# Second-kind layers: where the halves of the modulation shift are made, and how far the sums of squares follow the rest tiles

## The chip, the cores and the metric

One core of a Trainium2 chip runs the kernel. Its engines work in parallel, each through an instruction queue of its own, strictly in order: TensorE (PE) for matmuls, VectorE (DVE), ScalarE (ACT), GpSimd (POOL), and SyncE (SP), which issues the weight loads. They wait for each other through semaphores only. The metric is the time of one execution in microseconds (us) on the device.

## The reference

512 tokens of width 1024 pass through two layers of a first kind (differential and dilated attention, SwiGLU) and then two of a second kind, which are the ones concerned here:

```python
for l in range(DEPTH):                       # second_block
    mod = c_act @ w_mod[l] + b_mod[l]
    sh1, sc1, gt1, sh2, sc2, gt2 = jnp.split(mod[:, None, :], 6, axis=-1)
    h = rmsnorm(x, g_mix[l]) * (1.0 + sc1) + sh1
    z = h @ w_in[l]
    ...   # y_a pooling, y_b banded attention, y_c sparse attention (top 128 keys), y_d latent attention
    mix = group_rmsnorm(jnp.concatenate([y_a, y_b, y_c, y_d], axis=-1), g_group[l])
    x = x + gt1 * (mix @ w_out[l])
    h = rmsnorm(x, g_ffn[l]) * (1.0 + sc2) + sh2
    f = (jax.nn.silu(h @ ffn_w1[l]) * (h @ ffn_w3[l])) @ ffn_w2[l]
    x = x + gt2 * f
```

`sh2` is the modulation shift that the change is about. The sparse attention selects, for each query, the 128 keys with the highest index scores.

## The kernel before

Activations lie transposed, 128 features by 512 tokens a tile, eight tiles (`KT`) for the width of 1024. Each fp32 weight chunk of 128x1024 is loaded to a ring (`wring`), and split into a high part, copied by ACT (`cut_high`, L422), and a rest, made by POOL (`cut_rest`, L445: wring - wHi). Each product of `gemm` is then three matmuls, hHi x wHi, hHi x wLo and hLo x wHi (L470). ACT makes a high part as soon as the tile that used the buffer two chunks before is done (`follow`). PSUM results go in rings of two slots: `psG` (ring G), `psT` (T), and the two score slots of `psS` (ring S). A matmul into a slot first waits until the former content has been read (`is_free`).

A second-kind layer does the following, in this order, on every engine:

1. **Front.** Twelve tiles of z (`Z_FRONT`), among which the index scores are computed on PE, rectified on ACT (`index_relu`) and summed into `score` on DVE (`index_sum`, L2405). The last two front tiles hold values, which ACT copies to `vT` (L2094). Behind the front tiles ACT loads the table of the exponential (L2140).
2. **Mixing stage.** A loop over 29 steps, written out on each engine. In step s PE computes the scores of pair s (`scores`, L1854, two slots), transposes the probabilities of pair s-2 (L1869) and multiplies those of pair s-3 by the values (L1889); steps 0 to 4, 7 and 9 hold one more z tile each (`TILE_AT`). DVE adds the bias to the scores of pair s, with the row's minimum (`lowest`, L2466), which empties the slots; ACT takes the exponential (`expo`, L2152). Between these DVE does the selection: 48 rounds (`take`), each a top-8 search (L2412) and a replacement (L2413), nine of them ahead of step 0 (`TAKEN_FIRST`), the others spread over steps by a table (`TAKE_AT`). In step 7 DVE makes two reciprocals (`c_inv`, L2525), which PE spreads (L1949).
3. **Out tiles and rest tiles.** The product with `w_out` is split over k: "out" tiles over six of the eight k tiles, within the last steps, and eight "rest" tiles over the last two (six matmuls each), when the last attention output is there. DVE adds each result to `xT` (`add_out`, L2450). ACT squares each finished tile (`norm_act_squares`, L549, two buffers `sq`), and PE adds the squares of tile j up (`squares_of(j)`, L558) behind rest tile j+1.
4. **Shift row.** PE multiplies the shift with the first two weight chunks of the FFN (L1995, L1996), for which the shift stands in `shift` as two columns for each k: its high half, copied by ACT (L2219), and the remainder, subtracted by DVE (L2531).
5. **FFN.** Gate, up and down products, PE almost without a pause.

The copy and the subtraction stand, before the change, behind the mixing loop: on ACT behind the load of the square root's table (L2213), on DVE ahead of the first rest tile's add. `modc`, from which they are made, is ready at the layer's start.

Of the kernel before, what the change touches and what calls it, by code (L numbers as in the profile page):

```python
# [25 lines left out]
ACT = mybir.ActivationFunctionType  # L26
ALU = mybir.AluOpType
# [7 lines left out]
KT = DM // P  # L35
# [96 lines left out]
def head_pair(n):  # L132

    return n // (TT - 1), 1 + n % (TT - 1)
# [108 lines left out]
def program(nc, t, out):  # L243
    ctx = ExitStack()
    with ctx:
        def sb(name, shape, where=ctx, dtype=F32):
            return where.enter_context(nc.sbuf_tensor(name, shape, dtype))
# [8 lines left out]
        def sem(name):  # L256
            return ctx.enter_context(nc.semaphore(name))
# [26 lines left out]
        shift_full, shift_row, shift_col = sem("shift_full"), sem("shift_row"), sem("shift_col")  # L284
# [171 lines left out]
        def gemm(pe, u, c, rhs, kts, i=None, Ku=0, Kc=0, start=True, stop=True, ready=None, used=True, cut=None):  # L456

            pe.wait_ge(w_cut[c % CUTS], c // CUTS + 1 if i is None else i * (Kc // CUTS) + (c // CUTS + 1))
            if start:
                pe.wait_ge(*G.is_free(u, i, Ku))
            hi, lo = rhs
            wh, wl = (wHi[:, c % CUTS, :, :], wLo[:, c % CUTS, :, :]) if cut is None else cut
            for j, k in enumerate(kts):
                for n, (w, r) in enumerate(((wh, hi), (wl, hi), (wh, lo))):
                    if ready is not None and n != 1:
                        pe.wait_ge(*ready(j)[n // 2])
                    mm = pe.matmul(psG[:, G.slot(u), :], w[:, k, :], r(j),  # L470
                                   start=start and j == 0 and n == 0, stop=stop and j == len(kts) - 1 and n == 2)
            if used:
                mm.then_inc(G.filled(u) if stop else w_used, 1)
# [23 lines left out]
        def tiles(a, first=0):  # L497
            return lambda j: a[:, first + j, :]
# [56 lines left out]
        def quarter_sums(pe, tt, parts, start=True, stop=True):  # L555
            for a in range(TT):
                for j, s in enumerate(parts):
                    mm = pe.matmul(psT[32 * a:32 * a + 32, T.slot(tt), 0:P], ones[:, 0:32], s[:, a * P:(a + 1) * P],  # L558
                                   start=start and j == 0, stop=stop and j == len(parts) - 1)
            return mm  # L560
# [1132 lines left out]
        shift = sb("shift", [P, KT, 2], blk, F32R)  # L1693
# [3 lines left out]
        modc, gains = sb("modc", [P, MODS], blk), sb("gains", [P, 2, KT], blk)  # L1697
# [35 lines left out]
        for l in range(DEPTH):  # L1733
            with nc.Block() as block:
# [42 lines left out]
                def _(pe):  # L1777
# [196 lines left out]
                    def squares_of(j):  # L1974
                        if j == 0:
                            pe.wait_ge(*T.is_free(t_N2))
                        pe.wait_ge(sq_full, q_N2 + j + 1)
                        quarter_sums(pe, t_N2, (sq[:, (q_N2 + j) % 2, :],), j == 0, j == KT - 1)\
                            .then_inc(sq_used if j < KT - 1 else T.filled(t_N2), 1)
# [3 lines left out]
                    for j in range(KT):  # L1983
                        at = 2 * (j % 4)
                        gemm(pe, g[f"rest{j}"], CH2_WR + j // 4, (tiles(hHi, REST_K[0]), tiles(hLo, REST_K[0])), (at, at + 1))
                        if j >= 1:
                            squares_of(j - 1)

                    first = (wHi[:, CH2_GU % CUTS, :, :], wLo[:, CH2_GU % CUTS, :, :]), first_cuts[0]
                    pe.wait_ge(shift_full, 2)  # L1990
# [69 lines left out]
                def _(act):  # L2060
# [28 lines left out]
                    def tile(name):  # L2089
                        u = g[name]  # L2090
                        if name in (6, 15, 16):
                            n = (6, 15, 16).index(name)
                            act.wait_ge(*G.is_full(u))
                            act.activation(vT[:, n % 2, :], psG[:, G.slot(u), :], ACT.Copy).then_inc(vT_full, 1)  # L2094
                            act.wait_ge(vT_full, n + 1)
                            act.sem_inc(G.emptied(u), 1)
                        elif name == 7:
                            act.wait_ge(*G.is_full(u))
                            for b, out in ((0, ik), (64, sak)):
                                for at in (0, 64):  # L2100
                                    ins = act.activation(out[at:at + 64, :], psG[b:b + 64, G.slot(u), :], ACT.Copy)
                            ins.then_inc(G.emptied(u), 1)
                        else:
                            if name == 17:
                                act.wait_ge(scale_full, 1)
                            copy(name, place[name], scale=-0.125 if name in (11, 12, 17, 18) else 1.0)
                        follow(act, CH2_Z + z_pos[name], u)

                    def value_rows(name):
                        u = tr[name]  # L2110
                        act.wait_ge(*T.is_full(u))
                        if name == "v6":
                            s = psT[:, T.slot(u), :].rearrange("p (c d) -> p c d", c=TT)
                            act.activation(Vsa[:, :, 0:64], s[:, :, 0:64], ACT.Copy)
                            act.activation(iws[:, :, :], s[:, :, 64:64 + IDX_HEADS], ACT.Copy,
                                           scale=(IDX_HEADS ** -0.5) * (IDX_DIM ** -0.5)).then_inc(T.emptied(u), 1)
                        else:
                            hd = 0 if name == "v15" else 2
                            act.activation(Vca[:, :, hd:hd + 2, 0:64], psT[:, T.slot(u), :].rearrange("p (c h d) -> p c h d", c=TT, h=2),
                                           ACT.Copy).then_inc(T.emptied(u), 1)  # L2120

                    def index_relu(n):
                        nk = P * (head_pair(n // 2)[1] + 1)
                        act.wait_ge(*S.is_full(s_IDX + n))
                        if n >= 4:
                            act.wait_ge(relu_used, n - 3)
                        act.activation(relu[:, n % 4, 0:nk], psS[:, S.slot(s_IDX + n), 0:nk], ACT.Relu).then_inc(S.emptied(s_IDX + n), 1)

                    for at, name in enumerate(Z_ORDER[:Z_FRONT]):
                        first, second = INDEX_AT.get(at, (None, None))  # L2130
                        if first is not None:
                            index_relu(2 * first)
                            index_relu(2 * first + 1)
                        tile(name)
                        if at == 3:
                            value_rows("v6")
                        if second is not None:
                            index_relu(2 * second)
                            index_relu(2 * second + 1)
                    act.preload_act_table(ACT.Exp)  # L2140

                    def out_T(p):
# [30 lines left out]
                    for s in range(STEPS + 1):  # L2173
# [29 lines left out]
                        if s in (5, 6):  # L2203
                            j, name = s - 5, ("CQ", "CK")[s - 5]
# [10 lines left out]
                    def rough(j):  # L2215

                        act.activation(hHi[:, j, :], xT[:, j, :], ACT.Copy, scale=gains[:, 1, j:j + 1]).then_inc(rough_high, 1)

                    act.activation(shift[:, :, 0], modc[:, 3 * KT:4 * KT], ACT.Copy).then_inc(shift_full, 1)  # L2219

                    def added(j):
                        if j in (1, 2):
# [140 lines left out]
                def _(dve):  # L2363
# [66 lines left out]
                        did(dve.memset(score[0:CHUNK, qt - 1, P * (qt + 1) - CHUNK:P * (qt + 1)], NEG))  # L2430
                    dve.wait_ge(ca_in, 16)
                    did(dve.memset(T_tab[0:CHUNK, :, SEQ - CHUNK:SEQ], FAR))
                    taken = 0
                    for _ in range(TAKEN_FIRST):
                        take(taken)
# [91 lines left out]
                        if s in DONE_AT:  # L2527
                            mix(DONE_AT[s])
                    assert taken == ROUNDS * (TT - 1)
                    dve.wait_ge(shift_full, 1)  # L2530
                    dve.tensor_tensor(shift[:, :, 1], modc[:, 3 * KT:4 * KT], shift[:, :, 0], ALU.subtract).then_inc(shift_full, 1)  # L2531

                    def rough(j):

                        dve.wait_ge(rough_high, j + 1)
                        dve.scalar_tensor_tensor(hLo[:, j, :], xT[:, j, :], gains[:, 1, j:j + 1], hHi[:, j, :], ALU.mult, ALU.subtract)\
                           .then_inc(rough_rest, 1)
# [259 lines left out]
```

## Time and profile before

| | |
|---|---|
| median of the runs before | 3213.44 us (3209.69, 3213.44 and 3215.41) |
| the profiled execution | 3212.82 us, span of the trace 3211.0 us |
| busy share of the span | PE 98%, DVE 45%, ACT 42%, POOL 43% |
| mean granted TensorE clock | 0.996 of full speed |
| second-kind layers in the trace | about 1924 to 2564 us and 2564 to 3211 us |
| mixing stage, first of them | about 2013 to 2176 us; rest tiles from there to about 2195 us |

A row of a timeline has the start and the duration in us, the engine, the source line, the operation, the tile written and those read, the shape and a count; square brackets give the engine's idle time before it and what ended it. Starts and durations are those of one profiled execution.

### The profile page before, as it was taken

To read this page: it belongs to the slowest core of one execution; us is meant where nothing else is said; L and a number is where in the kernel's file an instruction comes from. 1 tells how busy PE (TensorE), PEld (TensorE's weight loads), DVE (VectorE), ACT (ScalarE), POOL (GpSimd) and SP (SyncE) were. 2 spreads that over 40 slices of the span, in tenths; PEclk is the share of its full clock that TensorE was granted. 3 is DMA by queue.
4 is the path that set the end of the run, shared out by engine and by line. 5 is a ranking of instruction groups with operands and counts; after the bars stand their busy time and mean duration, and the time that the engine had idled before them with its cause. 6 is when DMAs were issued, how large, how long until landed. Compare 5 with 4: busy or idle time off the path is not lost. (4 is left out here: it accounts for less than half of the span.)

```text
span 3211.0 us, 45072 instructions
## 1 busy us (share of the span) xinstructions
PE 3152.3 (98%) x15772; PEld 2527.8 (79%) x15772; DVE 1448.4 (45%) x2712; ACT 1362.3 (42%) x2133; POOL 1395.6 (43%) x687
## 2 busy tenths in 40 slices
PE   9999999999999999999999999999999999999999
PEld 7778888888887778888888876777888767778887
DVE  5753336655425733336655424854121148541211
ACT  6765554322227765554322224454222245542222
POOL 3233333655543233334655443544444435444444
PEclk9999999999999999999999999999999999999999
DMA  3122222355422122223355423112222331122232
GB/s 143 65 76 89 88 82 105 119 193 199 164 92 88 64 84 79 86 88 106 137 186 201 155 84 115 68 40 79 98 98 98 105 108 66 40 86 91 98 103 87
DMA packets 93599, 333.33 MB, mean 104 GB/s; under 512 B 10864, under 2 KB 12080, under 8 KB 93232
## 3 DMA queue, kind: packets, MB, share of 16 engines
q1 hardware_dynamic: 91760, 325.52, 29.0%
q10 hardware_dynamic: 1728, 6.36, 0.5%
q8 instruction: 66, 1.08, 0.1%
q14 instruction: 45, 0.37, 0.0%
HBM read 329.69 MB, written 8.44 MB: 105 GB/s over the span
## 5 line engine op out<-in xcount | busy, mean ns | idle before, releaser
L445 POOL TENSOR_TENSOR wLo<-wring,wHi 128x1024 fp32r<-128x1024 f32 x470 | 1170.5, 2491 | 1646.3 <-ACT wHi L422 1646.1
L470 PE MATMUL psG<-hHi,wHi 128*128 128x512 f32 x2880 | 1142.5, 397 | 6.4 <-DVE xT L2450 1.4
L470 PE MATMUL psG<-hLo,wHi 128*128 128x512 f32 x2880 | 1127.3, 391 | 4.1 <-POOL hLo L512 3.4
L470 PE MATMUL psG<-hHi,wLo 128*128 128x512 f32 x2880 | 1124.1, 390 | 0.0
L422 ACT ACTIVATE wHi<-wring 128x1024 fp32r<-128x1024 f32 x470 | 497.5, 1059 | 1077.8 <-PE psG L470 1070.5
L470 PEld LDWEIGHTS psG<-hHi,wHi 128*128 128x128 f32 x2880 | 542.1, 188 | 141.7 <-issue 28.2
L470 PEld LDWEIGHTS psG<-hLo,wHi 128*128 128x128 f32 x2880 | 541.6, 188 | 125.3 <-POOL hLo L512 11.4
L470 PEld LDWEIGHTS psG<-hHi,wLo 128*128 128x128 f32 x2880 | 542.6, 188 | 108.4 <-issue 0.5
L470 PE MATMUL psG<-hidLo,wHi 128*128 128x512 f32 x704 | 274.3, 390 | 0.0
L470 PE MATMUL psG<-hidHi,wLo 128*128 128x512 f32 x704 | 274.2, 390 | 0.0
L470 PE MATMUL psG<-hidHi,wHi 128*128 128x512 f32 x704 | 274.2, 390 | 0.0
L2598 DVE TENSOR_TENSOR psS<-tmp,psG 128x512 f32<-128x512 f32 x42 | 29.2, 696 | 345.6 <-PE psG L470 345.6
L1070 ACT ACTIVATE tmp<-psG 32x512 f32<-32x512 f32 x256 | 150.9, 590 | 24.3 <-PE psG L470 20.8
L470 PEld LDWEIGHTS psG<-hidHi,wHi 128*128 128x128 f32 x704 | 132.2, 188 | 27.8
L470 PEld LDWEIGHTS psG<-hidHi,wLo 128*128 128x128 f32 x704 | 132.2, 188 | 27.3
L470 PEld LDWEIGHTS psG<-hidLo,wHi 128*128 128x128 f32 x704 | 132.2, 188 | 27.2
L1559 DVE CUSTOM_DVE_ANT_0 modw<-modw,cb 128x1024 f32<-128x1024 f32 x96 | 130.8, 1362 | 5.1
L1509 DVE CUSTOM_DVE_ANT_0 soft<-psS,mask 128x768 f32<-128x768 f32 x64 | 61.0, 953 | 154.6 <-issue 154.6
L1394 DVE SCALAR_TENSOR_TENSOR ra<-psG,ropec 128x512 f32<-128x512 f32 x44 | 30.4, 692 | 215.2 <-ACT tmp L1070 215.2
L1571 DVE COPY branch<-psG 128x512 f32 x32 | 22.1, 692 | 190.8 <-PE psG L470 189.4
L2562 DVE SCALAR_TENSOR_TENSOR xT<-psG,modc,xT 128x512 f32 x16 | 12.0, 751 | 195.7 <-PE psG L470 195.7
L2252 ACT ACTIVATE tmp<-psG 128x512 f32<-128x512 f32 x40 | 23.9, 598 | 174.9 <-PE psG L470 174.9
(411 smaller groups left out, 3616.1 us busy)
## 6 DMA issues: line engine op xcount, KB each, us to landing
wring<-in_w SPq DMA_DIRECT2D x490, 512.0 KB, 3.2
modw<-in_wmod SPq DMA_DIRECT2D x96, 512.0 KB, 3.6
e_copies<-e_rows ACTq DMA_DIRECT2D x8, 512.0 KB
T_tab<-e_copies SPq DMA_DIRECT2D x4, 1024.0 KB, 5.5
mask<-in_mask SPq DMA_DIRECT2D x2, 1536.0 KB, 6.0
xin_sb<-in_x SPq DMA_DIRECT2D x4, 512.0 KB, 5.5
e_copies<-e_rows ACTq DMA_DIRECT2D x8, 256.0 KB
out<-o_sb SPq DMA_DIRECT2D x4, 512.0 KB, 2.6
```

Of the source, the lines that this page charges most:

```text
L422: act.activation(wHi[:, c % CUTS, :, :] if out is None else out[0], wring[:, c % RING, :, :], ACT.Copy).then_inc(w_high, 1)
L445: pool.tensor_tensor(lo, wring[:, c % RING, :, :], hi, ALU.subtract).then_inc(w_cut[c % CUTS], 1)
L470: mm = pe.matmul(psG[:, G.slot(u), :], w[:, k, :], r(j), start=start and j == 0 and n == 0, stop=stop and j == len(kts) - 1 and n == 2)
L1070: ins = act.activation(rot[32 * a:32 * a + 32, slot, :], ps[32 * b:32 * b + 32, :], ACT.Copy, scale=QSCALE[slot])
L1394: dve.scalar_tensor_tensor(ra[:, :], ps, QSCALE[slot], ropec[:, :], ALU.mult, ALU.mult).then_inc(emptied[0], 1)
L1509: dve.tensor_tensor_reduce(Sm[:, s, :], psS[:, S.slot(u), 0:DL_KEYS], mask[:, n // 2, :], 1.0, -3.0e38, ALU.add, ALU.max, stat[:, s, 0:1]) ...
L1559: dve.tensor_tensor_reduce(modw[:, j % 2, :], modw[:, j % 2, :], cb[:, :], 1.0, 0.0, ALU.mult, ALU.add, small[:, 9 + j % 4:10 + j % 4]).th ...
L1571: did(dve.tensor_copy(buf[:, i * 4 + j, :], ps))
L2252: act.activation(tmp[:, j, :], psG[:, G.slot(ga), :], ACT.Silu).then_inc(G.emptied(ga), 1)
L2562: dve.scalar_tensor_tensor(xk, psG[:, G.slot(g0 + j), :], modc[:, bass.ds(i * 4 + (col + j), 1)], xk, ALU.mult, ALU.add).then_inc(G.emptie ...
L2598: dve.tensor_tensor(hid, tmp[:, j, :], psG[:, G.slot(u), :], ALU.mult).then_inc(G.emptied(u), 1)
```

## The change

On ACT the copy of the shift's high half moves from behind the mixing loop to the place behind the front tiles, ahead of the exponential's table. On DVE the subtraction, with its wait for the copy, moves to the place behind the index sums, ahead of the nine first rounds of the selection. On PE the squares of tile j are added up behind rest tile j+2 in place of j+1; those of the last but one follow behind the last rest tile.

```diff
@@ PE
                     for j in range(KT):
                         at = 2 * (j % 4)
                         gemm(pe, g[f"rest{j}"], CH2_WR + j // 4, (tiles(hHi, REST_K[0]), tiles(hLo, REST_K[0])), (at, at + 1))
-                        if j >= 1:
-                            squares_of(j - 1)
+                        if j >= 2:
+                            squares_of(j - 2)
+                    squares_of(KT - 2)
@@ ACT
                             index_relu(2 * second)
                             index_relu(2 * second + 1)
+                    act.activation(shift[:, :, 0], modc[:, 3 * KT:4 * KT], ACT.Copy).then_inc(shift_full, 1)
                     act.preload_act_table(ACT.Exp)
...
-                    act.activation(shift[:, :, 0], modc[:, 3 * KT:4 * KT], ACT.Copy).then_inc(shift_full, 1)
-
                     def added(j):
@@ DVE
                     dve.wait_ge(ca_in, 16)
                     did(dve.memset(T_tab[0:CHUNK, :, SEQ - CHUNK:SEQ], FAR))
+                    dve.wait_ge(shift_full, 1)
+                    dve.tensor_tensor(shift[:, :, 1], modc[:, 3 * KT:4 * KT], shift[:, :, 0], ALU.subtract).then_inc(shift_full, 1)
                     taken = 0
                     for _ in range(TAKEN_FIRST):
                         take(taken)
                         taken += 1
...
                     assert taken == ROUNDS * (TT - 1)
-                    dve.wait_ge(shift_full, 1)
-                    dve.tensor_tensor(shift[:, :, 1], modc[:, 3 * KT:4 * KT], shift[:, :, 0], ALU.subtract).then_inc(shift_full, 1)
-
                     def rough(j):
```

DVE's queue at the end of the index sums, before the change: the last sum, the blanking of unreachable scores and table entries, and the first rounds of the selection, with the semaphores that each instruction waits for.

```order
1206 L2405 SCALAR_TENSOR_TENSOR score<-relu,iws,score 128x512 [waits relu_used,S_read1]
1207 L2430 MEMSET score 64x64 [waits relu_used]
1208 L2430 MEMSET score 64x64 [waits dve_did] x2
1209 L2432 MEMSET T_tab 64x4x64 [waits ca_in,dve_did]
1210 L2412 MAX top<-score 128x8 [waits dve_did]
1211 L2413 MATCH_REPLACE score<-top,score 128x256 [waits dve_did]
```

The same place of DVE's queue after the change:

```order
1206 L2405 SCALAR_TENSOR_TENSOR score<-relu,iws,score 128x512 [waits relu_used,S_read1]
1207 L2430 MEMSET score 64x64 [waits relu_used]
1208 L2430 MEMSET score 64x64 [waits dve_did] x2
1209 L2432 MEMSET T_tab 64x4x64 [waits ca_in,dve_did]
1210 L2434 TENSOR_TENSOR shift<-modc,shift 128x8 [waits shift_full,dve_did]
1211 L2412 MAX top<-score 128x8
1212 L2413 MATCH_REPLACE score<-top,score 128x256 [waits dve_did]
```

The subtraction (L2434), with its wait on `shift_full`, now stands ahead of every round of the selection.

ACT's queue behind the front tiles after the change (lines here are one higher than before): the last two value tiles, each followed by a weight cut, then the copy, the table and the first values and exponentials of the mixing stage. Before the change the same rows stand there without the copy.

```order
963 L2095 ACTIVATE sq<-psG 128x512 [waits G_full0]
964 L422 ACTIVATE wHi<-wring 128x1024 [waits vT_full,w_full0,G_full0]
965 L2095 ACTIVATE sq<-psG 128x512 [waits G_full1]
966 L422 ACTIVATE wHi<-wring 128x1024 [waits vT_full,w_full1,G_full1]
967 L2141 ACTIVATE shift<-modc 128x8
968 L2142 ACT_TABLE_LOAD
969 L2120 ACTIVATE Vca<-psT 128x4x2x64 [waits T_full0]
970 L2154 ACTIVATE Pm<-Sm,low 128x128 [waits S_read0]
```

The copy (L2141) waits for no semaphore of its own, and stands behind four instructions that wait for PE or for loads.

PE's queue after the second rest tile, as a difference (lines with - are before, with + after the change): the third rest tile (six L470 matmuls) and the first squares (L558).

```order
 L470 MATMUL psG<-hHi,wLo 128x512
 L470 MATMUL psG<-hLo,wHi 128x512
+L470 MATMUL psG<-hHi,wHi 128x512 [waits G_read1,w_cut1]
+L470 MATMUL psG<-hHi,wLo 128x512
+L470 MATMUL psG<-hLo,wHi 128x512
+L470 MATMUL psG<-hHi,wHi 128x512
+L470 MATMUL psG<-hHi,wLo 128x512
+L470 MATMUL psG<-hLo,wHi 128x512
 L558 MATMUL psT<-sq,ones 32x128 [waits sq_full,T_read0]
```

The third rest tile now stands ahead of the first squares; from there on each group of squares stands one tile later.

## Rows read from the trace of the kernel before

**Rows 1.** The page, busy time of each engine with its share of the span.

```profile
PE 3152.3 (98%) x15772; PEld 2527.8 (79%) x15772; DVE 1448.4 (45%) x2712; ACT 1362.3 (42%) x2133; POOL 1395.6 (43%) x687
```

**Rows 2.** Timeline of PE, first second-kind layer, rest tiles, squares and shift row.

```profile
2178.42 0.39 PE L470 MATMUL psG<-hHi,wLo 128*128 128x512 f32 x1
2178.64 0.39 PE L470 MATMUL psG<-hLo,wHi 128*128 128x512 f32 x1
2181.35 0.49 PE L558 MATMUL psT<-sq,ones 128*32 128x128 f32 x8 [2.32 <-ACT sq L549]
...
2187.07 0.50 PE L470 MATMUL psG<-hHi,wHi 128*128 128x512 f32 x1
...
2194.83 0.22 PE L1995 MATMUL psG<-wHi,shift 128*2 128x128 f32 x1
```

**Rows 3.** Timeline of DVE at the first rest tiles.

```profile
2178.97 0.92 DVE L2531 TENSOR_TENSOR shift<-modc,shift 128x8 fp32r<-128x8 f32 x1 [1.86 <-ACT shift L2219]
2179.80 1.40 DVE L2450 SCALAR_TENSOR_TENSOR xT<-psG,modc,xT 128x512 f32<-128x512 f32 x2
```

**Rows 4.** Timeline of ACT at the first rest tiles.

```profile
2177.43 1.28 ACT L2213 ACT_TABLE_LOAD   x1
2178.72 0.21 ACT L2219 ACTIVATE shift<-modc 128x8 fp32r<-128x8 f32 x1
2180.58 0.63 ACT L549 ACTIVATE sq<-xT 128x512 f32<-128x512 f32 x1 [1.64 <-DVE xT L2450]
```

**Rows 5.** Windows: busy time by engine (count), then granted clock, DMA share, GB/s.

```profile
2181.30:2185.10 3.80, 3.75 (x22) 2.21 (x22) 0.37 (x1) 1.65 (x3) 0.00 (x0) 0.55 0.33 129
```

**Rows 6.** Timeline of PE, second such layer, second rest tile and shift row.

```profile
2819.39 0.39 PE L470 MATMUL psG<-hLo,wHi 128*128 128x512 f32 x1
...
2835.60 0.22 PE L1995 MATMUL psG<-wHi,shift 128*2 128x128 f32 x1
```

**Rows 7.** Timeline of ACT behind the front tiles, first second-kind layer.

```profile
2012.85 0.60 ACT L2094 ACTIVATE sq<-psG 128x512 f32<-128x512 f32 x1 [3.61 <-PE psG L470]
...
2014.70 1.28 ACT L2140 ACT_TABLE_LOAD   x1
```

**Rows 8.** Timeline of DVE: first top-8 search, then the reductions of step 0.

```profile
2007.06 0.43 DVE L2412 MAX8 top<-score 128x8 f32<-128x256 f32 x1
...
2015.92 0.29 DVE L2466 CUSTOM_DVE_ANT_0 Sm<-psS,T_tab 128x128 f32<-128x128 f32 x1
...
2016.14 0.29 DVE L2466 CUSTOM_DVE_ANT_0 Sm<-psS,T_tab 128x128 f32<-128x128 f32 x1
```

**Rows 9.** Timeline of POOL at the first rest tiles.

```profile
2177.49 2.37 POOL L445 TENSOR_TENSOR wLo<-wring,wHi 128x1024 fp32r<-128x1024 f32 x1 [2.89 <-ACT wHi L422]
```

**Rows 10.** Timeline, POOL and DVE, a mask operation within the mixing stage.

```profile
2048.52 2.37 POOL L445 TENSOR_TENSOR wLo<-wring,wHi 128x1024 fp32r<-128x1024 f32 x1
...
2049.86 1.25 DVE L2415 TENSOR_SCALAR score<-score 128x384 f32<-128x384 f32 x1
```

**Rows 11.** Timeline of POOL at the end of the front.

```profile
2014.76 2.40 POOL L445 TENSOR_TENSOR wLo<-wring,wHi 128x1024 fp32r<-128x1024 f32 x1 [3.04 <-ACT wHi L422]
```

**Rows 12.** Timeline, DVE and PE, scores that wait for a reduction.

```profile
2077.07 0.28 DVE L2466 CUSTOM_DVE_ANT_0 Sm<-psS,T_causal 128x128 f32<-128x128 f32 x1
...
2077.51 0.49 PE L1854 MATMUL psS<-kn,qn 64*128 64x128 f32 x4 [0.82 <-DVE low L2466]
```

**Rows 13.** Timeline of PE: scores of step 1 in both second-kind layers.

```profile
2019.71 0.49 PE L1854 MATMUL psS<-cak,caq 64*128 64x128 f32 x4
...
2660.59 0.49 PE L1854 MATMUL psS<-cak,caq 64*128 64x128 f32 x4
```

**Rows 14.** Waits of DVE, 2004 to 2060: us in total, times, longest.

```profile
DVE Sm L2466 <- PE psS L1854: 1.6, 3, 1.0
```

**Rows 15.** Timeline, DVE and PE, step 7.

```profile
2057.02 1.75 DVE L2525 RECIPROCAL c_inv<-c_root 128x128 f32<-128x128 f32 x2
...
2058.39 1.95 PE L1949 MATMUL psT<-c_inv,spread 128*128 128x128 f32 x16
```

## The prediction

> **What bounds the kernel now.** The page comes first: TensorE (PE) is busy for 98% of the span [rows 1], so a change pays or costs only where PE stands still or runs at a lower clock. The chain that ended last runs through PE almost everywhere; in each second-kind layer it leaves PE where the rest tiles begin, and goes through a table load on ScalarE (ACT), the shift's subtraction on VectorE (DVE), the first rest tile's add and its square. So PE's timeline is read there next. The last matmul of the second rest tile starts at 2178.64, and PE does nothing until 2181.35, waiting for the first square [rows 2]. DVE's timeline says why: its queue is in order, the subtraction of L2531 stands ahead of the adds, begins only at 2178.97 and lets the first add start at 2179.80 [rows 3]. It waited for ACT's copy at 2178.72, which stood behind a 1.28 us table load [rows 4].
>
> The stall has a tail. In the 3.8 us behind it the granted clock is 0.55 of full speed [rows 5]: nearly all of that stretch is at 1.2 GHz, the lower of its two levels, and before the stall it was at 2.4.
>
> **What the rest stage gives back.** A rest tile is six matmuls, one per 0.22 to 0.23 us (2178.42 to 2178.64), 1.36 us; with its squares behind it the undisturbed period is (2194.83 - 2187.07) / 4 = 1.94 us [rows 2]. After the change the third rest tile follows the second at once, at 2178.64 + 0.23 = 2178.87. Six tiles and seven groups of squares are left ahead of the shift's matmuls: six periods and one group alone, 6 x 1.94 + 0.36 = 12.0 us, so these begin at 2190.87 and not at 2194.83: 3.96 us earlier. 2.48 of that is the stall, 1.48 the slow clock behind it. The second layer gives the same: 2819.39 + 0.23 + 12.0 = 2831.62 against 2835.60, 3.98 us [rows 6].
>
> Does anything else stop PE there? The first add can begin when its tile is full, six matmuls ahead of the second tile's end (2178.64 + 0.39 - 1.36 = 2177.7), and takes 0.7 (half of the 1.40 of two, [rows 3]); the square can begin when the table load ends, 2178.71, and the last one took from 2180.58 to PE's start at 2181.35, 0.77 us [rows 2, 4]. So the square is ready near 2179.5. With a lag of one tile PE would still wait 0.6 us; with two it asks only at 2180.2. The edit on PE is needed beside the move, and it costs no instruction. Later squares are asked for one tile later than now, and both buffers of squares come free in time, because the add takes longer than a group of squares. I take the whole 3.97 us a layer.
>
> **What the move costs.** The copy and subtraction now stand ahead of the mixing stage. ACT runs the copy behind all front tiles: behind the last value tile, for which it waits 3.61 us on PE, and behind that tile's weight cut. The next thing on ACT there now is the table load at 2014.70 [rows 7], so the copy takes its place and is done near 2014.9. DVE reaches the same point much earlier: its first top-8 search starts at 2007.06 [rows 8]. In the changed order the subtraction, with its wait, stands ahead of that search. So DVE, which is almost never idle in this stage, waits from 2007.06 to 2014.95: 7.9 us. Queued behind it are nine searches and then the two lowest-score reductions of step 0, and ACT's exponentials wait for those.
>
> Then the subtraction itself, 8 columns. Its row says 0.92 us [rows 3], far too much for its size, and it ends at 2179.89, 0.03 after the weight rest on GpSimd (POOL), which ran from 2177.49 to 2179.86 [rows 9]. The mask operation at 2049.86 likewise took 1.25 us and ended 0.2 us after POOL's operation [rows 10]. I read this as DVE held until POOL has finished. At the new place POOL's weight rest begins at 2014.76 and lasts to 2017.16 [rows 11], and it starts ahead of the subtraction by 0.1 to 0.2 us. So I let the subtraction end at 2017.19, and the next DVE instruction start 0.09 earlier, as in [rows 3]: 2017.10. DVE is late by D = 2017.10 - 2007.06 = 10.04 us. Were the 0.92 us its own length, D would be 8.7; were it free and short (0.15 us), 8.0.
>
> The Trainium skill (SBUF — State Buffer, "Who interferes with whom") says that a DVE instruction with two SBUF inputs and a GpSimd instruction that reads SBUF exclude each other, whichever starts first holding the shared ports to its end. By that page the subtraction waits for POOL's whole operation, as forecast (3222); by its row taken at face value the sum would be 3219.7. The two endings in [rows 3, 9] bear the page out.
>
> **Where PE pays.** The score tiles in PSUM are two, so the scores of step 1 may start only when both reductions of step 0 have read theirs. The second of these ends at 2016.14 + 0.29 = 2016.43 [rows 8], and PE starts 0.16 us after such an end (2077.07 + 0.28, then 2077.51) [rows 12]. PE comes to those scores at 2019.71 [rows 13], so 3.12 us of D are free, and the stall is 10.04 - 3.12 = 6.92 us. Behind it I expect a slow clock as in the rest stage, 1.5 us (bounds: none, and twice that): 8.4 us. Nothing else is on PE to fill it: the queue is in order.
>
> A second place checks this. Up to step 7 DVE waits for PE three times, 1.6 us in all [rows 14]; these waits absorb part of its lateness. At 2057.02 it begins two reciprocals (1.75 us), which PE's spread at 2058.39 needs [rows 15]; the first is ready about 0.3 us ahead. So PE must be at least D - 1.6 - 0.3 = 8.1 us late there, a floor under the 8.4. After it DVE and PE are shifted together, and ACT, POOL and the weight loads follow. No wait in the rest of the stage is for a transfer, so nothing takes the delay back. In the second layer PE comes to the same scores at 2660.59 [rows 13], 640.88 later, and the neighbours repeat to the hundredth.
>
> **The sum.** Per layer 8.4 - 3.97 = +4.45; two layers, +8.9 us. The profiled execution took 3212.82 us (span 3211.0): 3221.7. The median of the runs shown, 3213.44, is 0.6 above it: **3222**. The bounds: the clock's tail none, then the floor holds, 2 x (8.1 - 3.97) = +8.2, 3221.6; the tail twice, 2 x (9.9 - 3.97) = +11.9, 3225.3. As one measurement of this kernel tells about 0.2% (6.4 us) from no change, this is slower by 0.28%, not far beyond that.
>
> **The rivals.**
> - *The subtraction is not held by POOL.* D = 8.0 to 8.7 gives a loss of D - 1.62 = 6.4 to 7.1 us a layer, net +4.9 to +6.3: 3218.3 to 3219.7, within 0.2%. For it: no row shows this instruction beside an idle POOL; POOL leads by only 0.1 to 0.2 us. Against it: the two endings.
> - *The wait costs PE nothing, and only the gain stays.* DVE would have to find the copy done. One mechanism decides it, when ACT reaches the copy: it needs nothing but `modc`, so only its place in ACT's queue makes it late. PE pays nothing if D is below 2.0 us, and gain and loss meet at D - 1.62 = 3.97, D = 5.6. Against it: ACT's row at 2012.85 waits for PE, and the copy stands behind it in the order. Then 3213.4 - 7.9 = 3205.5.
> - *The gain does not come.* If the first squares find another wait (the table load is still there), only the loss stays: 3213.4 + 16.8 = 3230. For it: the square now comes free only 0.7 us ahead of PE. Against it: no row of that stretch is later than I counted.
>
> **How the numbers follow.** Forecast 0.64, POOL not holding 0.18, wait free 0.07, gain missing 0.05; the remaining 0.06 is for sums between these, most of them within 0.2%. The range runs from the second case to the forecast's upper bound with some two microseconds for the scatter of single runs: 3217 to 3227. Slower by over 0.2%: 0.64 + 0.05 and a share of the rest, 0.71; within 0.2%, 0.21; faster, 0.08.
>
> **What would show it.** In the changed profile: at the rest tiles, no wait of PE for a square, granted clock 1.00, and 12.0 us from the third rest tile to the shift's matmuls. On DVE, idle time of some 7.9 us ahead of the subtraction, released by ACT's copy, and the subtraction ending with POOL's operation. On PE, some 6.9 us of waiting ahead of the scores of step 1, released by DVE, and a slow clock behind it. I am wrong if DVE shows no idle time there, if PE's wait in step 1 is under 4 us, or if PE waits for a square or for POOL's weight rest in the rest stage.

## The result and the profile after

The changed kernel takes 3221.03 us, the median of 7 runs (3219.36 to 3228.62), against 3210.7 us for the kernel before in its 7 runs beside it (3207.94 to 3215.41). The ratio is 1.0032, with a 95% interval of 1.0023 to 1.0042: 7 to 13 us slower. The prediction was 3222 us.

The profiled execution took 3219.36 us (span 3217.6 us). The busy times on its page:

```profile
PE 3151.4 (98%) x15772; PEld 2526.7 (79%) x15772; DVE 1450.3 (45%) x2712; ACT 1362.4 (42%) x2133; POOL 1396.1 (43%) x687
```

Beside [rows 1] there is nothing to see in it: the same matmuls, the same busy shares. The change is worth a few us in each of two places of a layer, and only the timeline of those places shows it. First the start of the mixing stage of the first second-kind layer, chosen rows of all engines in order of time, the last row from the second layer. In brackets is the idle time ahead of an instruction, and what ended it.

```profile
2005.58 0.27 DVE L2432 MEMSET T_tab<- 64x256 f32 x1
2012.44 1.06 ACT L422 ACTIVATE wHi<-wring 128x1024 fp32r<-128x1024 f32 x1 [0.17 <-ACT sq L2095]
2013.40 0.19 ACT L2141 ACTIVATE shift<-modc 128x8 fp32r<-128x8 f32 x1
2013.58 2.40 POOL L445 TENSOR_TENSOR wLo<-wring,wHi 128x1024 fp32r<-128x1024 f32 x1 [3.05 <-ACT wHi L422]
2013.70 2.30 DVE L2434 TENSOR_TENSOR shift<-modc,shift 128x8 fp32r<-128x8 f32 x1 [7.85 <-ACT shift L2141]
2015.92 0.42 DVE L2412 MAX8 top<-score 128x8 f32<-128x256 f32 x1
...
2024.76 0.29 DVE L2468 CUSTOM_DVE_ANT_0 Sm<-psS,T_tab 128x128 f32<-128x128 f32 x1
2024.98 0.28 DVE L2468 CUSTOM_DVE_ANT_0 Sm<-psS,T_tab 128x128 f32<-128x128 f32 x1
2025.42 0.80 PE L1854 MATMUL psS<-cak,caq 64*128 64x128 f32 x4 [6.82 <-DVE low L2468]
...
2033.45 0.70 PE L1854 MATMUL psS<-cak,caq 64*128 64x256 f32 x4
...
2669.72 0.80 PE L1854 MATMUL psS<-cak,caq 64*128 64x128 f32 x4 [6.83 <-DVE low L2468]
```

DVE is through with its small tasks at 2005.85 and stands idle for 7.85 us, until ACT's copy at 2013.40. Its subtraction of 8 columns then takes 2.30 us and ends at 2016.00; POOL's weight rest, begun 0.12 us ahead of it, ends at 2015.98. The engines were said above to wait for each other through semaphores only; the subtraction waits for no semaphore of POOL's, and yet ends with POOL's operation. Such a hold shows as the instruction's own duration and not as idle time ahead of it. The searches begin at 2015.92, the reductions of step 0 end 13.26 us behind the start of that step's scores (at 2012.00) where it was 3.25 us before, and PE stands for 6.82 us ahead of the scores of step 1 (6.83 in the second layer). In the kernel before these scores followed without a wait [rows 13].

What the clock does there is in the windows (length; busy time and instructions of PE, its weight loads, DVE, ACT and POOL; granted clock; DMA share; GB/s):

```profile
2018.50:2025.40 6.90, 0.10 (x1) 0.01 (x1) 6.45 (x24) 0.30 (x1) 0.00 (x0) 0.82 0.01 5
2025.40:2029.40 4.00, 3.98 (x12) 3.10 (x13) 3.72 (x13) 2.30 (x5) 2.11 (x1) 0.50 0.00 0
2029.40:2033.00 3.60, 3.60 (x17) 2.95 (x16) 3.39 (x15) 0.69 (x2) 0.27 (x1) 0.96 0.42 146
```

For 4 us behind the wait the clock is 0.50, the lower level of 1.2 GHz, and then nearly all 2.4 GHz. From the scores of step 1 to those of step 2 it is 8.03 us (2025.42 to 2033.45), against the 6.09 of the kernel before (from 2019.71 in [rows 13]):

```profile
2025.80 0.70 PE L1854 MATMUL psS<-cak,caq 64*128 64x256 f32 x4
```

The other place is the rest tiles, 160 us on:

```profile
2186.32 0.39 PE L470 MATMUL psG<-hHi,wHi 128*128 128x512 f32 x1
...
2187.45 0.39 PE L470 MATMUL psG<-hLo,wHi 128*128 128x512 f32 x1
2187.77 0.43 PE L558 MATMUL psT<-sq,ones 128*32 128x128 f32 x8
...
2197.53 0.64 PE L558 MATMUL psT<-sq,ones 128*32 128x128 f32 x16
2198.10 0.22 PE L1996 MATMUL psG<-wHi,shift 128*2 128x128 f32 x1
...
2842.77 0.22 PE L1996 MATMUL psG<-wHi,shift 128*2 128x128 f32 x1
```

```profile
2187.00:2200.00 13.00, 13.00 (x122) 8.66 (x120) 7.17 (x10) 9.14 (x14) 8.05 (x4) 1.00 0.37 127
```

The first group of squares follows the rest tile without a wait, where it had one of 2.32 us [rows 2]; PE is busy for 13.00 of 13.00 us at a clock of 1.00, where [rows 5] had 0.55. From the start of the third rest tile (2186.32) to the shift's matmuls it is 11.78 us. The time that the change was to free is free.

**Sizes from place to place.** Two executions, even of one kernel, reach this stage up to 3 us apart, ahead of the changed instructions (the scores of step 0 begin at 2012.00 and 2015.03 in the two profiled executions of the changed kernel), so times since the start can't be compared. Three events of a layer can: A, the scores of step 0, ahead of all that the change touches; B, the matmul with the last wait ahead of the rest tiles; C, the first of the shift's matmuls. These are A and B of both layers before:

```profile
2013.18 0.49 PE L1854 MATMUL psS<-cak,caq 64*128 64x128 f32 x4
...
2171.97 0.47 PE L470 MATMUL psG<-hHi,wHi 128*128 128x512 f32 x1 [0.72 <-DVE xT L2450]
...
2654.07 0.49 PE L1854 MATMUL psS<-cak,caq 64*128 64x128 f32 x4
...
2812.73 0.47 PE L470 MATMUL psG<-hHi,wHi 128*128 128x512 f32 x1 [0.72 <-DVE xT L2450]
```

and after:

```profile
2012.00 0.49 PE L1854 MATMUL psS<-cak,caq 64*128 64x128 f32 x4
...
2179.41 0.47 PE L470 MATMUL psG<-hHi,wHi 128*128 128x512 f32 x1 [0.72 <-DVE xT L2452]
...
2656.29 0.49 PE L1854 MATMUL psS<-cak,caq 64*128 64x128 f32 x4
...
2824.10 0.47 PE L470 MATMUL psG<-hHi,wHi 128*128 128x512 f32 x1 [0.72 <-DVE xT L2452]
```

From A to B it was 158.79 and 158.66 us, and is 167.41 and 167.81: 8.62 and 9.15 us lost. From B to C it was 22.86 (2194.83 in [rows 2]) and 22.87, and is 18.69 and 18.67: 4.17 and 4.20 won. Net +9.4 us. All experiments below are measured with the same three events.

### The profile page after: what moved, and what is told of

It reads as the page before. It is cut to its first block and busy times, and to the rows that moved or that the text cites. A ratio compares the mean times of both kernels' runs of the same rounds, so it can differ in the third digit from the quotient of the medians.

```text
span 3217.6 us, 45074 instructions
## 1 busy us (share of the span) xinstructions
PE 3151.4 (98%) x15772; PEld 2526.7 (79%) x15772; DVE 1450.3 (45%) x2712; ACT 1362.4 (42%) x2133; POOL 1396.1 (43%) x687
## 3 DMA queue, kind: packets, MB, share of 16 engines
HBM read 329.69 MB, written 8.44 MB: 105 GB/s over the span
## 5 line engine op out<-in xcount | busy, mean ns | idle before, releaser
L470 PE MATMUL psG<-hHi,wHi 128*128 128x512 f32 x2880 | 1142.1, 397 | 6.1 <-DVE xT L2452 1.4
L470 PE MATMUL psG<-hLo,wHi 128*128 128x512 f32 x2880 | 1126.6, 391 | 2.9 <-POOL hLo L512 2.2
L470 PE MATMUL psG<-hHi,wLo 128*128 128x512 f32 x2880 | 1123.6, 390 | 0.0
L470 PEld LDWEIGHTS psG<-hHi,wHi 128*128 128x128 f32 x2880 | 542.5, 188 | 141.5 <-issue 27.0
L470 PEld LDWEIGHTS psG<-hLo,wHi 128*128 128x128 f32 x2880 | 541.8, 188 | 124.3 <-POOL hLo L512 9.9
L470 PEld LDWEIGHTS psG<-hHi,wLo 128*128 128x128 f32 x2880 | 543.0, 189 | 109.4 <-issue 0.5
L470 PE MATMUL psG<-hidLo,wHi 128*128 128x512 f32 x704 | 273.9, 389 | 0.0
L470 PE MATMUL psG<-hidHi,wHi 128*128 128x512 f32 x704 | 273.9, 389 | 0.0
L470 PE MATMUL psG<-hidHi,wLo 128*128 128x512 f32 x704 | 273.9, 389 | 0.0
L470 PEld LDWEIGHTS psG<-hidHi,wHi 128*128 128x128 f32 x704 | 132.1, 188 | 28.0
L470 PEld LDWEIGHTS psG<-hidLo,wHi 128*128 128x128 f32 x704 | 132.1, 188 | 27.5
L470 PEld LDWEIGHTS psG<-hidHi,wLo 128*128 128x128 f32 x704 | 132.1, 188 | 27.0
```

Source lines behind the costliest of these rows:

```text
L470: mm = pe.matmul(psG[:, G.slot(u), :], w[:, k, :], r(j), start=start and j == 0 and n == 0, stop=stop and j == len(kts) - 1 and n == 2)
```

## The experiments

The theory, as the prediction has it: the gain is that of the rest stage, needs the move and the lag together, and is 4 us a layer; the loss is DVE's lateness at the first searches (the wait for the copy, and the subtraction held by POOL), of which 3.12 us are free at the scores of step 1; a slow clock behind the wait adds to it. The rivals: the lag alone makes the gain; the early place costs whatever DVE waits for; the copy ahead of the table load costs; what costs is any lateness, in proportion or as such; the slow clock is not part of it. Seven kernels follow; the kernel before ran beside the first four at 3212.74 us (20 runs), and beside the last three at 3212.63 us (26 runs).

**lag_only: the edit on PE alone.** The kernel before, and

```diff
-                        if j >= 1:
-                            squares_of(j - 1)
+                        if j >= 2:
+                            squares_of(j - 2)
+                    squares_of(KT - 2)
```

> The kernel before with the squares two tiles behind and nothing else: copy and subtraction stay at their old place. My theory: the square of the first tile stays as late as it was, since the subtraction ahead of the add still waits for the table load and the copy, and the third rest tile now needs a slot that only this add frees. The stall ahead of the squares (2.48 us a layer) goes for the most part to a wait of some 1.8 us ahead of the third rest tile; with the slow clock behind it kept, the kernel gains 0.7 to 2.2 us a layer: 3206 to 3209 us against 3210.7 before, hardly to be told from no change. Rival, the lag by itself is the gain (4 us a layer): 3202 to 3203 us.

Measured: 3207.33 us, ratio 0.9983 (0.9974 to 0.9992). Its timeline at the third rest tile:

```profile
2177.99 2.37 POOL L445 TENSOR_TENSOR wLo<-wring,wHi 128x1024 fp32r<-128x1024 f32 x1 [2.88 <-ACT wHi L422]
2179.47 0.92 DVE L2532 TENSOR_TENSOR shift<-modc,shift 128x8 fp32r<-128x8 f32 x1 [1.86 <-ACT shift L2220]
2180.30 1.40 DVE L2451 SCALAR_TENSOR_TENSOR xT<-psG,modc,xT 128x512 f32<-128x512 f32 x2
...
2181.19 0.47 PE L470 MATMUL psG<-hHi,wHi 128*128 128x512 f32 x1 [1.66 <-DVE xT L2451]
...
2182.74 0.43 PE L558 MATMUL psT<-sq,ones 128*32 128x128 f32 x8
```

```profile
2182.00:2186.00 4.00, 4.00 (x30) 2.53 (x29) 1.96 (x3) 3.29 (x6) 0.07 (x1) 1.00 0.30 116
```

The wait has moved from the squares to the tile, whose slot the late add frees, as expected. Behind 1.66 us the clock stays at 1.00, where the lower end of the expectation had a slow clock. B to C is 20.54 us in both layers: 2.32 won, just over what was expected, and not the rival's 4 (its 8 us in all lie just at the end of the interval, and the trace decides against it). The lag alone is a little over half of the gain, and it costs nothing elsewhere.

**move_only: the move alone.** The changed kernel, and

```diff
-                        if j >= 2:
-                            squares_of(j - 2)
-                    squares_of(KT - 2)
+                        if j >= 1:
+                            squares_of(j - 1)
```

> The changed kernel with the squares one tile behind, as before: only the halves of the shift are moved. My theory: DVE's wait for the copy and TensorE's wait behind it at the scores of step 1 are as in the changed kernel (8.6 to 9.1 us lost a layer), and the rest stage keeps most of its gain, because the add no longer stands behind the subtraction: TensorE waits some 0.6 us a layer for the first square. So about 3222 us, 1 us over the changed kernel. Rival, the lag makes the gain and the move only costs: the rest stage waits as it did, and the time is 3228 to 3229 us.

Measured: 3224.3 us, ratio 1.0040 (1.0027 to 1.0054).

```profile
2188.44 0.42 PE L558 MATMUL psT<-sq,ones 128*32 128x128 f32 x8 [0.47 <-ACT sq L549]
```

```profile
2188.40:2192.40 4.00, 3.96 (x32) 2.51 (x36) 1.12 (x2) 2.28 (x4) 0.42 (x1) 1.00 0.39 135
```

PE waits 0.47 us for the first square (0.6 was foreseen), the clock behind it is 1.00, and B to C is 19.52 us: 3.34 won, so the move has most of the gain by itself, and the lag adds 0.84 to it. A to B is 167.25 and 168.37: 8.46 and 9.71 lost, the second more than expected. That makes 11.5 us in all, and 11.6 by the medians, where 3222 against 3210.7 was 11.3. The rival (17 to 18 us) lies at the upper end of the interval, 17.3, but it has PE wait for the square as before, and the 0.47 us decide against it.

**copy_early: only ACT's copy at another place.** The changed kernel, and

```diff
                     shifted(0, 0)
+                    act.activation(shift[:, :, 0], modc[:, 3 * KT:4 * KT], ACT.Copy).then_inc(shift_full, 1)
...
-                    act.activation(shift[:, :, 0], modc[:, 3 * KT:4 * KT], ACT.Copy).then_inc(shift_full, 1)
                     act.preload_act_table(ACT.Exp)
```

> The changed kernel with ACT's copy at the start of the layer's ACT program, behind the first shifted tile, where the modulation has long been there; DVE's subtraction stays where the change put it. My theory (the loss is DVE's wait for ACT's copy, and what held the subtraction was GpSimd's operation that happened to run beside it): DVE finds the copy done and goes on at once, the subtraction takes 0.1 to 0.2 us if GpSimd is idle then (0.92 us, as in the kernel before, if not), TensorE doesn't wait ahead of the scores of step 1 beyond what it did before, and only the gain of the rest stage is left, 8.2 to 8.4 us in both layers: 3202.5 us, ratio 0.9974 to the kernel before. Rival (an early place costs by itself, whatever DVE waits for: the sixteen rounds and the first step are late or the ring of scores is upset in another way): 3215 us or more.

Measured: 3202.72 us, ratio 0.9970 (0.9957 to 0.9982).

```profile
2006.13 0.27 DVE L2432 MEMSET T_tab<- 64x256 f32 x1
2006.44 0.17 DVE L2434 TENSOR_TENSOR shift<-modc,shift 128x8 fp32r<-128x8 f32 x1
2006.52 0.42 DVE L2412 MAX8 top<-score 128x8 f32<-128x256 f32 x1
2008.69 2.40 POOL L445 TENSOR_TENSOR wLo<-wring,wHi 128x1024 fp32r<-128x1024 f32 x1 [4.63 <-ACT wHi L422]
...
2019.09 0.49 PE L1854 MATMUL psS<-cak,caq 64*128 64x128 f32 x4
```

The same subtraction, at the same place of DVE's queue as in the changed kernel, takes 0.17 us with POOL idle around it, DVE doesn't wait, and PE reaches the scores of step 1 without one. A to B is back at 158.60 us, B to C at 18.67. With the copy moved, the loss is gone and the gain stays: this kernel beats both.

**sub_late: only DVE's subtraction at another place.** The changed kernel, and

```diff
-                    dve.wait_ge(shift_full, 1)
-                    dve.tensor_tensor(shift[:, :, 1], modc[:, 3 * KT:4 * KT], shift[:, :, 0], ALU.subtract).then_inc(shift_full, 1)
                     taken = 0
...
+                        if s == 0:
+                            dve.wait_ge(shift_full, 1)
+                            dve.tensor_tensor(shift[:, :, 1], modc[:, 3 * KT:4 * KT], shift[:, :, 0], ALU.subtract).then_inc(shift_full, 1)
```

with the added lines behind the reductions of step 0.

> The changed kernel with DVE's wait and subtraction behind the first step's score reductions in place of ahead of the first rounds; ACT's copy stays where the change put it. My theory: DVE comes to the wait at about 2016.3 us, when the copy is done (2013.6), so that only GpSimd's operation can hold the subtraction, for 0.8 us at most, which is less than the 1.97 us that were free: no loss, the gain of the rest stage alone, 3202.5 to 3203.5 us. Rival (the copy itself on ACT, ahead of the table load for the mixing stage, makes the loss): 3211 us or more, and nothing like copy_early's time.

Measured: 3203.74 us, ratio 0.9974 (0.9964 to 0.9984).

```profile
2015.29 2.40 POOL L445 TENSOR_TENSOR wLo<-wring,wHi 128x1024 fp32r<-128x1024 f32 x1 [3.04 <-ACT wHi L422]
...
2016.88 0.83 DVE L2524 TENSOR_TENSOR shift<-modc,shift 128x8 fp32r<-128x8 f32 x1
```

The copy stands where the change put it, ahead of the table load, and costs nothing: A to B is 158.92 us. The subtraction is held again, to 2017.71, 0.02 us past the end of POOL's operation at 2017.69; 0.8 us of lateness are within what is free. So the loss lies in the meeting of the two places, not in either.

**dose: another lateness, with no wait.** copy_early, and

```diff
-                    did(dve.memset(T_tab[0:CHUNK, :, SEQ - CHUNK:SEQ], FAR))
+                    for _ in range(20):
+                        did(dve.memset(T_tab[0:CHUNK, :, SEQ - CHUNK:SEQ], FAR))
```

> copy_early (no wait for the copy) with nineteen more of DVE's memsets of 0.27 us ahead of the subtraction: they write what the first has written, and make DVE some 5.2 us late where the wait made it 10.04 us late. My theory (3.12 us of lateness are free at the scores of step 1, and a floor of the lateness less 1.97 us stands behind it): TensorE waits some 2.1 us there, the loss with a small tail is 3.2 to 3.6 us a layer against a gain of 4.2, so that the kernel is 1 to 2 us faster than before and 6.5 to 7.5 us slower than copy_early: about 3209 to 3210 us. Rival one, no slack: the loss is in proportion to the lateness, 4.5 to 4.8 us a layer, and the time 1 us over before, 3212 us. Rival two, what costs is that DVE is late for the step at all, whatever the size: 3219 us.

Measured: 3215.4 us, ratio 1.0010 (1.0001 to 1.0019). That is 2.8 us over the kernel before, where 1 to 2 us below it were expected.

```profile
2006.13 7.55 DVE L2433 MEMSET T_tab<- 64x256 f32 x20
...
2023.30 0.49 PE L1854 MATMUL psS<-cak,caq 64*128 64x128 f32 x4 [4.15 <-DVE low L2469]
...
2030.99 0.70 PE L1854 MATMUL psS<-cak,caq 64*128 64x256 f32 x4
```

Its window behind the wait, at a clock of 0.57:

```profile
2023.30:2027.30 4.00, 4.00 (x13) 3.15 (x14) 3.72 (x13) 2.28 (x5) 2.13 (x1) 0.57 0.00 0
```

The dose was larger than meant. The memsets start 0.38 us apart, 0.27 of work and 0.11 of idle time, so that twenty of them take 7.55 us; the subtraction adds 0.09. So DVE is 7.37 us late (memset to first search 7.67, against 0.30 before) and not 5.2. With this lateness PE's wait should be 7.37 - 3.12 = 4.25 us, and it is 4.15; in the changed kernel it should be 10.04 - 3.12 = 6.92, and it is 6.82. That is two doses on one line, both 0.1 below the reckoning: a us of lateness past 3.12 is a us of PE's time at that place. A to B is 5.78 and 5.90 us longer than before, 0.0 to 0.1 over the lateness less the 1.6 us that DVE's own waits absorb [rows 14]. Lateness as such (3219) is out; so is proportion to the whole lateness, which would be a wait of 7.37 x 6.82 / 10.04 = 5.0 us.

**awake and after_again: the tail.** The changed kernel, and ahead of the scores of step 1

```diff
+                        if s == 1:
+                            pe.wait_ge(*G.is_free(g[TILE_AT[1]]))
+                            keep_awake(pe, 28, psG[:, G.slot(g[TILE_AT[1]]), 0:P])
```

where `keep_awake` issues matmuls with the identity, into a slot whose next tile overwrites them. The changed kernel itself ran beside it.

> The changed kernel with 28 more matmuls (about 0.24 us each at full clock) ahead of the scores of step 1, in the PSUM slot of the tile that follows and before it is written, so that TensorE works through most of its 6.8 us of waiting; DVE's wait is as long as in the changed kernel. My theory (behind the wait TensorE's granted clock is near its lower level for some 4 us, and that is the tail of 1.94 and 2.33 us a layer): the clock stays near full and the tail goes, about 4 us in all: 4 us less than the changed kernel run beside it, some 3217 us. Rival (the tail is not the clock's, but scores and tiles that are late for another reason, and the waiting alone is the loss): no less than the changed kernel, or more, by as much as the matmuls last over the wait.

> The changed kernel as it is, beside the others on one chip, to compare them with: 3219 to 3223 us, 8 to 11 us over the kernel before.

Measured: awake 3220.63 us, ratio 1.0024 (1.0015 to 1.0033); the changed kernel beside it 3222.19 us, ratio 1.0029 (1.0019 to 1.0038). The added work gained 1.6 us by the medians, in intervals that overlap, and not the 4 that were expected. The timeline and a window of awake:

```profile
2020.05 6.42 PE L570 MATMUL psG<-ident 128*128 128x128 f32 x56
2027.04 0.49 PE L1854 MATMUL psS<-cak,caq 64*128 64x128 f32 x4 [0.57 <-DVE low L2471]
...
2033.15 0.70 PE L1854 MATMUL psS<-cak,caq 64*128 64x256 f32 x4
...
2057.64 1.13 PE L1854 MATMUL psS<-cak,caq 64*128 64x512 f32 x4 [0.77 <-DVE low L2471]
2061.62 1.13 PE L1854 MATMUL psS<-cak,caq 64*128 64x512 f32 x4 [0.85 <-DVE low L2471]
```

```profile
2027.00:2033.10 6.10, 6.06 (x28) 4.75 (x28) 5.72 (x22) 3.02 (x7) 2.42 (x1) 1.00 0.13 36
```

and the same scores in the changed kernel beside it, with the window behind its wait:

```profile
2028.45 0.80 PE L1854 MATMUL psS<-cak,caq 64*128 64x128 f32 x4 [6.82 <-DVE low L2468]
2037.28 0.70 PE L1854 MATMUL psS<-cak,caq 64*128 64x256 f32 x4
```

```profile
2028.40:2034.00 5.60, 5.55 (x15) 4.33 (x16) 5.24 (x20) 2.87 (x7) 2.38 (x1) 0.50 0.09 11
```

The tail is the clock's: with PE at work through the wait the clock is 1.00, and steps 1 to 2 take 6.11 us in place of 8.83 (8.03 in the other execution of the changed kernel). But PE then meets DVE, which is still late, at later scores (0.77 and 0.85 us of waiting that neither kernel had there), and A to B is 167.23 and 167.26 us: 8.44 and 8.60 lost, 0.2 to 1.0 less than in the two executions of the changed kernel. So my expectation failed on a point that the prediction had: there is a floor under the loss, and of the tail only what lies above it was won.

## Why the prediction came out right, step by step

**The gain, 3.97 us a layer.** Right: 4.17 and 4.20 from B to C, no wait for a square, the clock at 1.00. The 0.2 us more come from the stretch of 12.0 us, which is 11.78: its first tile takes 1.45 us to its squares, having none ahead of it, and its last two groups, side by side, 0.57, where the sum has 1.58 (1.94 - 0.36) and 0.72 (2 x 0.36). The prediction's price for a lag of one tile (PE waiting 0.6 us) was right too: 0.47 in move_only. That both edits are needed for the whole gain is shown: 2.32 for the lag, 3.34 for the move, 4.18 for both. With that the rival that the gain does not come is out.

**DVE's lateness, 10.04 us.** Right in both parts. The wait for the copy was to be 7.9 us and is 7.85. The subtraction was to end with POOL's operation, and did, 0.02 us past it, at 2.30 us. The rival that its 0.92 us were its own length is out: beside POOL it took 0.92 ([rows 3], and lag_only again), 0.83 and 2.30 us, ending 0.02 to 0.03 past POOL's end each time, and 0.17 us with POOL idle. The rule of the Trainium skill that the prediction named (SBUF — State Buffer, "Who interferes with whom") says that whoever starts first keeps the shared ports to its end; the trace agrees, with a lead of POOL's of only 0.12 us (2013.58 against 2013.70).

**PE's wait, 6.92 us at the scores of step 1.** Right: 6.82, and 4.15 at the smaller dose. The rival that the wait is free is out. copy_early and sub_late show that nothing else in the early place costs.

**The slow clock behind it, 1.5 us.** Right that it is there and that it adds to the wait, and too small: 1.94 and 2.33 in the profiled execution, 2.74 and 2.29 in the other. At the scores of step 2 PE is 8.84 and 9.23 us late (6.89 and 6.90 at those of step 1), and at B it is 8.62 and 9.15. So in the changed kernel the wait and the slow stretch, less 0.1 to 0.2, are the loss. The prediction's other reckoning, DVE's lateness less what DVE's own waits for PE absorb, is a floor, as it said: 10.04 - 1.6 = 8.4. The changed kernel lies above it, and DVE still waits for PE there, 0.3 us up to 2060 in place of the 1.6 of [rows 14]:

```profile
DVE Sm L2468 <- PE psS L1854: 0.3, 1, 0.3
```

awake shows the floor: without the slow stretch the loss is 8.44 and 8.60 us, and DVE has no such wait left. In dose both reckonings come to 5.8 (PE is 4.22 late behind the wait and loses 1.6 by the slow stretch; 7.37 - 1.6), so it can't tell them apart. The prediction took a further 0.3 off its floor for a reserve at the reciprocals, which awake doesn't show: PE meets DVE at scores ahead of them. So in these runs the loss is the larger of the two and not a sum of them, and the forecast's term of 1.5 us was 0.4 to 1.2 too small for the changed kernel.

**The sum.** +8.9 us forecast, +9.4 by the trace, +10.3 by the medians. That 3222 is within 1 us of the measured 3221.03 is partly luck: the forecast stood on 3213.44 us, 2.7 above the median of the runs beside the changed kernel, and its difference was 1.4 too small. The same accounting holds for every kernel run (A to B in each layer against before, B to C in both layers together, their sum, and the difference of the medians with the interval from the ratio):

| kernel | A to B, us | B to C, us | sum, us | measured, us |
|---|---|---|---|---|
| after | +8.62, +9.15 | -8.37 | +9.4 | +10.3 (7 to 13) |
| after_again | +9.41, +9.07 | -8.39 | +10.1 | +9.6 (6 to 12) |
| move_only | +8.46, +9.71 | -6.69 | +11.5 | +11.6 (9 to 17) |
| awake | +8.44, +8.60 | -8.40 | +8.6 | +8.0 (5 to 11) |
| dose | +5.78, +5.90 | -8.37 | +3.3 | +2.8 (0 to 6) |
| lag_only | -0.01, 0.00 | -4.65 | -4.7 | -5.4 (-8 to -3) |
| sub_late | +0.13, -0.05 | -8.36 | -8.3 | -9.0 (-12 to -5) |
| copy_early | -0.19, -0.11 | -8.39 | -8.7 | -10.0 (-14 to -6) |

What lies above the floor differs between two executions of one kernel (8.62 and 9.41 in the same layer), and the traces show by what: the stretch at 1.2 GHz behind PE's wait. In the six layers of after, after_again and move_only it lasted 3.7 to 6.3 us (in windows of 0.1 us) behind a wait of 6.82 or 6.83, and PE lost 1.7 to 2.9 us by it, 0.45 to 0.46 us for each us. Why its length differs stays open; no run tells what decides it.

## What to carry to other kernels

When a small step is moved out of a critical stretch, look up the time at which its input is ready at the new place, not only what the step costs: here 8 columns on DVE took 0.17 us where the copy was done and GpSimd idle, and made DVE 10 us late where ACT's queue had not come to the copy (7.85 us) and GpSimd had started just ahead (2.30 us). A step whose input is ready from the start of a layer belongs where its producer runs early, or behind the consumer that the next engine waits for; either kept the gain (8 to 10 us) without the loss. And before a stall's parts are added up, look for the engine that stays late all the while: PE's slow clock behind the wait was real, but taking it away moved part of the wait to a later place, and won only 0.2 to 1.0 us a layer.

## What the runs showed of the hardware beyond that

- In a chain of twenty memsets of 64 x 256, in which each one waits for the one before, each took the same 0.27 us as one alone, but they started 0.38 us apart, with 0.11 us of idle time between.
- What the granted clock did behind a wait of PE's: behind 0.47 and 1.66 us it stayed at 1.00 (move_only, lag_only); behind the 2.32 us of [rows 2] it was 0.55 over 3.8 us, behind 4.15 us 0.57 over 4 us (dose), and behind 6.82 us 0.50 over 4 us (after) and over 5.6 us (after_again). So the slow stretch is not of one length behind one and the same wait.
- One call of `keep_awake`'s matmul is two instructions in the trace (28 calls, x56), 0.115 us each.
